# Modulation summed inside the attention, one query quarter behind the first group of experts, and the expert choice in two halves between row products

## The reference

```
# PEER, for a chunk of 128 tokens xc (h already normed)
q = (xc @ w_query).reshape(128, 8, 2, 128)
s = einsum('chpd,hpnd->chpn', q, sub_keys)
s1, i1 = top_k(s[:, :, 0], 16);  s2, i2 = top_k(s[:, :, 1], 16)
best, flat = top_k(s1[..., :, None] + s2[..., None, :], 16)   # of 256 sums
experts = i1[flat // 16] * 128 + i2[flat % 16]
g = softmax(best)
act = gelu(einsum('cd,chkd->chk', xc, u[experts]))
out = einsum('chk,chkd->cd', g * act, v[experts])

# second block, for each of three sublayers
mod = silu(c) @ w_ada + b_ada              # shift, scale, gate of 1024 each
x = rmsnorm(h) * (1 + scale) + shift;  h = h + gate * sublayer(x)
```

## Time and profile before

| | us |
|---|---|
| median of 3 timed runs | 1658.79 |
| lowest and highest | 1653.77, 1662.54 |
| the profiled execution: its time | 1661.61 |
| its span | 1659.9 |

### The profile page before, as it was taken

One profiled execution on the slowest core, in us unless ns is written; L12 is line 12 of the kernel. 1 busy time (PEld: TensorE's weight loads), 2 busy tenths in 40 slices (PEclk: granted clock), 3 DMA queues, 4 the chain that ended last, 5 costly groups with the idle time before them and its releaser, 6 DMA issues.

```text
span 1659.9 us, 17494 instructions
## 1 busy us (share of the span) xinstructions
PE 1256.0 (76%) x6397; PEld 908.0 (55%) x6397; DVE 1024.9 (62%) x1899; ACT 407.9 (25%) x725; POOL 569.8 (34%) x626
## 2 busy tenths in 40 slices
PE   6987986487745554655465548999979889999997
PEld 4455762144522221222222226999869889789996
DVE  5767466776376667575655554677656554456655
ACT  1246113111012000110110003343334451144332
POOL 4100045565466676567677673101010000000000
PEclk9987987787878777777777779999989999999999
DMA  9832177798698999899999998778747435337561
GB/s 333 321 128 102 52 273 296 280 366 312 256 337 338 360 367 372 343 361 375 346 381 367 364 363 294 261 265 280 264 156 242 135 113 193 127 104 226 176 203 64
DMA packets 179709, 435.45 MB, mean 262 GB/s; under 512 B 13881, under 2 KB 84610, under 8 KB 179638
## 3 DMA queue, kind: packets, MB, share of 16 engines
q0 software_dynamic: 84384, 306.26, 49.0%
q1 hardware_dynamic: 94214, 126.18, 22.9%
q10 hardware_dynamic: 1040, 2.10, 0.4%
HBM read 433.44 MB, written 2.14 MB: 262 GB/s over the span
## 4 chain that ended last, share of the span: by engine, by line
PE 54%; DVE 12%; DMA 11%; POOL 11%; issue 9%; ACT 2%; another core or an unknown queue 1%; SPq 0%; DVEq 0%; POOLq 0%; ACTq 0%
PE quad L1389 13%; POOL arena L734 7%; PE quad_a L1343 7%; PE quad_a L1403 6%; PE quad_a L1470 5%; PE quad L1343 5%; DMA arena<-in_peer_v_dram,arena 4%; POOL ring L734 4%; PE quad_a L1209 4%; PE quad_a L1111 3%; DMA ring<-in_peer_v_dram,arena 2%; DMA ring<-in_peer_u_dram,arena 2%; PE quad_a L1538 2%; PE quad L1189 2%; PE quad_a L1528 2%
## 5 line engine op out<-in xcount | busy, mean ns | idle before, releaser
L1343 PE MATMUL quad_a<-arena 128*128 128x512 f32 x384 | 198.6, 681 | 161.4 <-DMA arena<-in_peer_v_dram,arena 161.4
L1343 PE MATMUL quad<-ring,arena 128*128 128x512 f32 x360 | 187.1, 682 | 123.9 <-DMA ring<-in_peer_v_dram,arena 108.9
L1343 PEld LDWEIGHTS quad_a<-arena 128*128 128x128 f32 x384 | 83.5, 222 | 275.8 <-issue 275.8
L734 POOL DMA_INDIRECT ring<-in_peer_u_dram,arena x136 | 138.9, 1021 | 245.0 <-DVE arena L1917 130.5
L1389 PE MATMUL quad<-u_hi,w_hi 128*128 128x256 f32 x704 | 200.4, 285 | 4.7 <-DVE u_lo L1837 4.7
L1343 PEld LDWEIGHTS quad<-ring,arena 128*128 128x128 f32 x360 | 77.8, 221 | 229.4 <-issue 229.4
L1389 PE MATMUL quad<-u_lo,w_hi 128*128 128x256 f32 x704 | 200.5, 285 | 0.0
L1389 PE MATMUL quad<-u_hi,w_lo 128*128 128x256 f32 x704 | 200.4, 285 | 0.0
L1937 DVE CUSTOM_DVE_ANT_0 arena<-ring,quad 128x1024 f32<-128x1024 f32 x128 | 154.6, 1220 | 61.0 <-DMA ring<-in_peer_u_dram,arena 45.1
L1805 DVE TENSOR_TENSOR w_lo<-ring,w_hi 128x2048 fp32r<-128x2048 f32 x66 | 150.7, 2290 | 67.3 <-ACT w_hi L918 66.9
L686 POOL DMA_DIRECT2D arena<-in_w_ada_dram x60 | 31.8, 531 | 454.6 <-DVE arena L1598 449.7
(11 more groups left out here) (307 smaller groups left out, 2165.9 us busy)
## 6 DMA issues: line engine op xcount, KB each, us to landing
ring<-in_ffn_w_gu_dram SPq DMA_DIRECT2D x44, 1024.0 KB, 9.0
arena<-in_w_ada_dram POOLq DMA_DIRECT2D x60, 512.0 KB, 6.1
ring<-in_ffn_w_down_dram SPq DMA_DIRECT2D x22, 1024.0 KB, 5.0
ring<-in_w_mix_in_dram SPq DMA_DIRECT2D x20, 1024.0 KB, 6.1
arena<-in_peer_w_query_dram SPq DMA_DIRECT2D x4, 2048.0 KB, 7.8
ring<-in_w_ada_dram POOLq DMA_DIRECT2D x12, 512.0 KB, 10.4
arena<-in_w_in_dram SPq DMA_DIRECT2D x3, 2048.0 KB, 36.2
arena<-in_w_out_dram SPq DMA_DIRECT2D x2, 2048.0 KB, 10.7
```

The lines of the kernel that those rows point to most:

```text
L734: gp.indirect_dma_start(out=rows_of(n), out_offset=None, in_=t["peer_" + kind][0], in_offset=bass.IndirectOffsetOnAxis(ap=expert[tt][:, sl ...
L1343: last = te.matmul(sum_side[tt][:, cols], diag[:, i % DIAGS], rows_of(n)[:, cols], start=(slot == pe_slots[0]), stop=(slot == pe_slots[-1] ...
```

## The change

- `modulation_first` puts the three partition sums of the first sublayer into the attention: columns behind the scores of step 0, half 0 behind the turned heads of step 1, half 1 behind those of step 2. ScalarE takes them in the same steps. `a_jobs` has them there.
- `query(0, 3)` and `key_scores(0, 3)` move behind `sum_group(0)`; ScalarE takes them behind `gelu_group(1)`.
- `NORM1_AT` goes from 2 to 1.
- `pick` is cut into `pick_rows` and `pick_cols` (no instruction added or removed). VectorE makes the dots first + 2 to first + 4, then top_keys and pick_rows, then the last three dots, then pick_cols and normalize.

```
-        NORM1_AT, QUERY1_AT = 2, 3
+        NORM1_AT, QUERY1_AT = 1, 3
...
-        for n in range(2):
+        for n in range(4):
             a_jobs += [("pq", 0, n), ("ps", 0, n)]
-        a_jobs += [("ada", job) for job in ADA_JOBS]
-        a_jobs += [("pq", 0, 2), ("pq", 0, 3), ("ps", 0, 2), ("ps", 0, 3)]
...
@@ ScalarE @@
+                if i == 0:
+                    evac(("ada", "columns"), lambda b: [(mod[:, 0, 0:2], b[:, 0:2 * KD].rearrange("p (m k) -> p m k", m=2))])
...
                 if i in LATER:
                     evac_heads(*LATER[i])
+                    half = slice((i - 1) * 512, i * 512)
+                    evac(("ada", i - 1), lambda b: [(gates[0][:, half], b[:, :])], scale=0.5)
...
             soft(0)
-            for job in ADA_JOBS:
...
             sc_e.wait_ge(d_free.sem, len(d_jobs))
             hn_in_psum.mark(ac.activation(hn_side[0], hn[0], ACT.Copy))
-            for what, n in (("pq", 2), ("pq", 3), ("ps", 2), ("ps", 3)):
-                evac_query(what, 0, n)
+            evac_query("pq", 0, 2)
+            evac_query("ps", 0, 2)
...
                 gelu_group(group)
+                if group == 1:
+                    evac_query("pq", 0, 3)
+                    evac_query("ps", 0, 3)
                 if group == NORM1_AT:
                     root(("h1", 1))
...
@@ TensorE @@
+            def modulation_first(job):
+                pe.wait_ge(ada_used.sem, ada_count(0, False))
+                a_full.mark(over_partitions(a_bank(("ada", job)), 0, job))
...
                     values(i - 3)
+                if i == 0:
+                    modulation_first("columns")
                 if 1 <= i < 5:
                     turn_keys(i - 1)
                 if i in LATER:
                     turn_heads(*LATER[i])
+                    modulation_first(i - 1)
...
-            pe.wait_ge(ada_used.sem, ada_count(0, False))
-            for job in ADA_JOBS:
-                bank = a_bank(("ada", job))
-                a_full.mark(over_partitions(bank, 0, job))
             query(0, 2)
-            query(0, 3)
             key_scores(0, 2)
-            key_scores(0, 3)
...
                 sum_group(group)
+                if group == 0:
+                    query(0, 3)
+                    key_scores(0, 3)
...
@@ VectorE @@
-            def pick(piece):
+            def pick_rows(piece):
...
                 row_of(per_head(e_hi)[:, hs], nh)
+
+            def pick_cols(piece):
...
                 if group < QT * GROUPS:
-                    dot_rows(tt, range(first + 2, first + GB))
+                    dot_rows(tt, range(first + 2, first + 5))
                 if group in KEYS_AT:
                     top_keys(*KEYS_AT[group])
                 if group - 1 in ROUTE_AT:
-                    pick(ROUTE_AT[group - 1])
+                    pick_rows(ROUTE_AT[group - 1])
+                if group < QT * GROUPS:
+                    dot_rows(tt, range(first + 5, first + GB))
+                if group - 1 in ROUTE_AT:
+                    pick_cols(ROUTE_AT[group - 1])
                     normalize(ROUTE_AT[group - 1])
```

More of the change, by code:

```diff
@@ L416, in program @@
         LATER = {1: TURNS[3], 2: TURNS[4]}
-        a_jobs += [(which + "T", tt, n) for which, tt in TURNS[:3] for n in range(2)]
+        ADA_JOBS = ("columns", 0, 1)
+        a_jobs += [(which + "T", tt, n) for which, tt in TURNS[:3] for n in range(2)] + [("ada", "columns")]
         for i, (tt, g) in enumerate(STEPS):
@@ L421, in program @@
             if i + 1 in LATER:
-                a_jobs += [(LATER[i + 1][0] + "T", LATER[i + 1][1], n) for n in range(2)]
+                a_jobs += [(LATER[i + 1][0] + "T", LATER[i + 1][1], n) for n in range(2)] + [("ada", i)]
             if i:
@@ L425, in program @@
         a_jobs += [("pT", 7, m) for m in maps(STEPS[7][1])]
-        ADA_JOBS = ("columns", 0, 1)
         ADA_BANK = {"columns": 2, 0: 3, 1: 2}
-        for n in range(2):
+        for n in range(4):
             a_jobs += [("pq", 0, n), ("ps", 0, n)]
-        a_jobs += [("ada", job) for job in ADA_JOBS]
-        a_jobs += [("pq", 0, 2), ("pq", 0, 3), ("ps", 0, 2), ("ps", 0, 3)]
         a_jobs += [("hnT", 1, b) for b in range(2)]
@@ L1263, in values, with over_partitions @@
                 d_full.mark(last)
+            def over_partitions(bank, s, job):
+                if job == "columns":
+                    for col in range(2 * KD):
+                        m, k = divmod(col, KD)
+                        last = te.matmul(bank[:, col:col + 1], ada_sum[s][m][:, k * P:(k + 1) * P], ones[:, 0:1], start=True, stop=True)
+                    return last
+                return te.matmul(bank[:, :], ones, ada_sum[s][2][:, job * 512:(job + 1) * 512], start=True, stop=True)
+            def modulation_first(job):
+                pe.wait_ge(ada_used.sem, ada_count(0, False))
+                a_full.mark(over_partitions(a_bank(("ada", job)), 0, job))
             pe.wait_ge(a_free.sem, a_at["kT", 2, 1] + 1)
@@ L1289, in _ @@
             values(7)
[L1291 to L1298, removed]
             pe.wait_ge(hn_ready.sem, 1)
@@ L1890, in row_of @@
                 step(v.tensor_tensor(dst, some[:, :, 0], some[:, :, 1], ALU.add))
-            def pick(piece):
+            def pick_rows(piece):
                 tt, h0, nh = PIECES[piece]
                 hs, cols = slice(h0, h0 + nh), slice(TOPK * h0, TOPK * (h0 + nh))
-                p_, lo_, hi_, n_, flat_, col_ = (tab[:, cols] for tab in (pos, e_lo, e_hi, slot_n, flat, col_u))
-                found, rows16, cols16 = hits[:, 0:nh], pos16[:, 0:nh], col16[:, 0:nh]
+                p_, flat_ = pos[:, cols], flat[:, cols]
+                found, rows16 = hits[:, 0:nh], pos16[:, 0:nh]
                 v.tensor_copy(rows16, per_head(flat)[:, hs])
@@ L1904, in pick @@
                 row_of(per_head(e_hi)[:, hs], nh)
+            def pick_cols(piece):
+                tt, h0, nh = PIECES[piece]
+                hs, cols = slice(h0, h0 + nh), slice(TOPK * h0, TOPK * (h0 + nh))
+                p_, lo_, hi_, n_, flat_, col_ = (tab[:, cols] for tab in (pos, e_lo, e_hi, slot_n, flat, col_u))
+                found, cols16 = hits[:, 0:nh], col16[:, 0:nh]
                 step(v.tensor_scalar(lo_, p_, 16.0, 8.0, ALU.is_ge, ALU.mult))
@@ L1964, in _ @@
             top_pairs(0)
-            pick(0)
+            pick_rows(0)
+            pick_cols(0)
             top_keys(0, 1)
```

## The result

| | median us | lowest, highest | runs |
|---|---|---|---|
| kernel before, same chip | 1656.15 | 1650.11, 1666.02 | 20 |
| changed kernel | 1664.93 | 1655.55, 1672.06 | 20 |

The ratio is 1.0053 [1.0037, 1.0069]; 1656.2 against 1658.79 was 0.9984. So this pair of profiles shows no loss, and cannot: the one after is 3.7 us under its kernel's median, the one before 5.5 over that of the 20 runs here.

The account below looks back on a forecast made before the run. The bound was DMA fetching of expert rows, so how early GpSimd issues each set. Terms +1.3 - 2.9 - 1.0 = -2.6 took the profiled 1661.61 to 1659.0; the timed median's 2.8 less gave 1656.2 us, range 1646 to 1667.

Parts of the forecast that it names:

- Step 1: Modulation sums moved into the attention: GpSimd's first set goes later, +1.3 us, bounds 0 and 7.0.
- Step 2: Quarter 3 behind group 0: GpSimd never stops early on; v0 row 2 at 239.4 against 256.94, 17.5 us won.
- the rival that quarter 3 is starved of instructions: Query quarter 3 takes 14 us instead of 7.4 through issue gaps; sum +4.0, 1662.8 us; chance 0.14.
- Step 3: Group 1: second tile's norm waits for ScalarE's root behind quarter 3; u2 row 3 goes 3.8 us later.
- X: GpSimd's issue of u2 row 3, at 268.12 us before; forecast 271.9 without the first set's shift.
- Step 4: Group 2 without the norm: u3 row 4 earlier than before, taken as -2.9 us, between -3.7 and -2.0.
- Step 5: Other groups, keys and picks before last dots: v rows 5 to 7 held some 4 us, additions earlier; -1.0 us together.
- The rival of the late dots: In six top_keys groups, v rows 5 to 7 wait 4 us unabsorbed; sum +10.4, 1669.2 us; chance 0.13.

Follow-up runs that it names:

- lot 2: One chip without issue gaps, before 1606.69 us: kernel before unchanged 0.9994, changed kernel 1.0135, modulation alone 0.9963, modulation and quarter 3 moved without a hold 0.9963.
- the third run of the picks: Kernel before with only pick_rows ahead of the last three dots, top_keys behind all dots, timed a third time: 0.9988.
- lot 4: One chip with gaps, before 1665.79 us: kernel before with picks only 0.9957, keys only 1.0011, whole split 1.0010; changed kernel 1.0040.
- lot 3: One chip, before 1659.41 us: picks only 0.9964, keys only 1.0039; modulation, norm and picks with quarter 3 moved without a hold 0.9957, with it unmoved 0.9955.
- the keys: Kernel before with only top_keys ahead of the last three dots, the whole pick behind all dots: 1.0039, on another chip 1.0011.
- lot 5: One chip with gaps, before 1656.51 us: kernel before with picks only 0.9988; with modulation, norm and picks changed, quarter 3 unmoved, 0.9962.

## Why the prediction was wrong, step by step

**Step 1, the modulation: the shift was about right, its sum was not.** The +1.3 us is the shift of GpSimd's first set alone. In the first pair of profiles this is 0.2 us, but one pair does not size it: over nine profiles with the modulation in its old place the first set goes at 216.3 us on average (213.3 to 218.1), over eleven with it in the attention at 218.6 (215.7 to 221.0), about 2.3 later, give or take 1.7. The columns that I put at 3.7 us take 6.83 at the granted clock of 0.50. For the whole part by itself 4 to 6 us won were expected, and -0.37% was measured, some 6 us, on a chip without gaps. Where this gain arises the profiles hardly show: that kernel's profiled run has a longer span than that of the unchanged one (1602.1 against 1598.6), against their medians, while from the first set to the last it has 723.1 us against 729.6.

**Step 2, the front: right where the quarters are whole.** Forecast for v0 row 2, with the shift, 240.7; it went at 240.9 on the chip of lot 2. On the first chip it went at 249.2: the rival that quarter 3 is starved of instructions named the right fault and the wrong quarter. Quarter 2 met the gaps, and ScalarE took it at 242.63 instead of some 231. Quarter 3 took 7.31 us, at a DMA share of 0.26. That this is why it was whole is not shown: a quarter in the third run of the picks (350.79 to 358.10) was whole too, at a share of 0.95. Nor does any trace say that the gaps are missing instructions; "issue" is only time without a visible wait.

**Step 3, the hold: the mechanism was right, X was mis-sized, and this is the step that failed.** The order was as forecast: sum of group 0, quarter 3, evictions, table load, root, scaling, addition, set. X was forecast at 273.2 with the shift and came at 276.9 (281.1 in lot 4). On the first chip this set is thus 8.8 us later than in the kernel before (8.6 without the shift), where the forecast had 5.1 (3.8 without it). The 3.7 us that X is behind its forecast were lost ahead of quarter 3: the sum of group 0 starts at 248.25 instead of 245.3 and ends at 262.4 instead of 258.2; from there to X it took 14.5 us, and I had 15.0 (the root starts 0.01 us behind the 1.28 of its table load, as in the row that I went by). On the chip of lot 2 X came at 274.9, close to the forecast, but there the kernel before has no gaps to lose and is at this set at 259.3: 15.5 us, of which 3.5 stand there from the first set on. I read the 268.12 of before as the place that the order of work gives; part of it was the gaps in the quarters. The price by runs: the change without its split is 1.0089, the same with ScalarE's root and masks ahead of the quarter 0.9963. The two stand in different lots, both on chips without gaps; the difference of 1.26% is some 20 us, more than the 15.5 that one pair of profiles shows. The profiles of these two kernels put u2 row 3 at 276.0 and 261.2, and the last set at 959.5 and 950.2.

**Step 4: right to 0.1 us.** From X to u3 row 4 I had 23.4 us (22.2 and one issue); it took 23.5 (276.88 to 300.38). The norm is gone from it, and the pick runs (285.45 to 296) but holds nobody: the second addition behind it waits 2.69 us for its v row. The gaps of the pick that I had half counted did not recur, which gives 0.8 back. The sum of steps 1 to 4 was still -1.6 forecast against +1.3 in the profiles: X is 3.7 later than forecast, less this 0.8. One term had a wrong reason: the 1.93 us of an issue do not come from the wait before it. The issue at 256.94 lasted 0.94 after 11.75 us. In the profile of before, all seven issues released by an addition took 1.93 or more and all seven released by other work of VectorE 1.03 or less; why is not shown. X is released by an addition, so its term was right all the same.

**Step 5: the hold right, what it gives back depends on the chip.** Held "some 4 us" in six groups was the forecast; the six took 3.1 to 4.0, 21.7 us together (17.4 on the chip of lot 2). The credit was the additions, which are late in the kernel before: 18.7 us of waits on them from 300 to 1010 us on the first chip, only 7.2 on the chip of lot 2. Where they are late, the split costs 0.10% [-0.15, +0.35], which does not contradict my -1.0 us. Where they are not, it costs 0.43% [0.19, 0.67]. That the late additions make this difference is a reading of the profiles; no run isolates it. The rival of the late dots thus has its mechanism shown, at half its price or less. The sign of its two halves is shown in lot 3: the keys cost, the picks do not. In lots 4 and 5 the picks again did not cost, but the keys' 1.0011 [0.9992, 1.0030] is not clear of nothing.

The parts as measured add up roughly. On chips without gaps: the change without its split +0.89% (in it the modulation's -0.37 and the hold's 1.26) and the split +0.43 make +1.3%, and the changed kernel measured +1.35. On chips with gaps no pair of runs differs in the hold alone. But the version of lot 3 with root and masks ahead of the quarter and the keys behind the dots is 0.9957, where the changed kernel, in other lots, is 1.0053 and 1.0040; less what the keys cost alone (0.39 and 0.11%), an estimate of 0.4 to 0.9% is left for the hold, 7 to 14 us, with the 8.8 us of the profiles in it.

So the step that failed is the price of the hold: 3.8 us in the sum, 8.6 in the first pair's profiles, and more where the kernel before has no gaps. The sum also had a base with one profile in it. Of the 11.4 us between -2.6 forecast and +8.8 measured, that pair shows 2.9 up to u3 row 4; from there on its changed kernel even gains, to 4.8 us ahead at the last set. By its own last test (the last set between 995 and 1010; it was 999.2) the forecast would have stood, while the medians of 20 runs say 8.8 us slower; in lot 4 the changed kernel's last set went at 1017.0.

## What to carry to other kernels

When a step is moved behind another one, look at what the consuming engine has queued behind its evictions: here a root and two masks behind a quarter's copy-out turned a front 7 to 8 us earlier into one 9 to 16 us later, and the other order on ScalarE took that loss away (1.0089 to 0.9963). Work put ahead of the last dots is free up to the slack of the buffer's next set and no further: half a pick fits, a 6 us search does not, so split work by its length. And read a stretch that shows "issue" gaps as two prices, with them and without, before counting what an edit there wins.

## What the runs showed of the hardware

The same program takes 1605 us on two chips and 1656 to 1666 on the others (one of them 1665.79 in lot 4 and 1656.51 in lot 5), and the last set of experts is issued at 943.2 us on one of the former against 1004.0. "issue" gaps of up to 1.8 us between matmuls of the query quarters were seen on those others only, 8 to 32 us a profile, in all twelve; they do not cover the difference. Nearly all of it lies between the first and the last set, with VectorE and GpSimd as long busy in both and the DMA share lower on the slower chip. Columns as the earlier trace rows; first the kernel before on the first chip, then on the chip of lot 2:

```profile
216.83:1004.02 787.19, 466.09 (x1254) 230.72 (x1254) 490.72 (x1102) 108.74 (x280) 509.90 (x513) 0.78 0.92 344
```

```profile
213.53:943.17 729.64, 457.33 (x1255) 224.91 (x1255) 490.40 (x1102) 109.10 (x280) 509.70 (x514) 0.79 0.98 372
```

The gaps are not TensorE's alone: from 300 us to the last set GpSimd has 145.8 us of "issue" on the first chip against 113.2 (0.35 us a time against 0.31, longest 1.3 and 0.6), VectorE 26.3 against 3.7. What makes them no run shows. The Trainium skill ("Runtime: NRT & Kernel Launch", Instruction fetch mechanics) says that the sequencer fetches ahead by a DMA queue of its own and calls the cost of crossing a block mostly hidden. The profiles of the 1605 us chips agree, with no such gap at the query products in all eight of them; if the gaps of the other chips are fetches, which is not shown, those do not.

Single executions stood up to 13.5 us from their kernel's median (the changed kernel in lot 2: 1613.87 profiled, 1627.39 median), more than all that was to be explained.
